# Input convolution of a two-layer decoder step: part of the taps moved from VectorE and TensorE to ScalarE and GpSimd

## The reference, cut to what matters

```python
def conformer_conv(h, buf, w_in, w_dw, b_dw, ln_g, ln_b, w_out):
    a, gate = jnp.split(h @ w_in, 2, axis=-1)
    u = a * jax.nn.sigmoid(gate)
    u, tail = causal_depthwise_conv(u, buf, w_dw, b_dw)   # width 31, 1024 channels
    u = layernorm(u, ln_g, ln_b)
    return jax.nn.silu(u) @ w_out, tail
```

## Time and profile before

| | us |
|---|---|
| median of 3 runs (lowest, highest) | 1561.69 (1561.35, 1566.02) |
| the profiled execution's own time | 1561.86 |
| its span, first to last instruction | 1560.1 |
| TensorE busy | 1502.1 (96%) |
| VectorE busy | 1014.5 (65%) |
| ScalarE busy | 879.0 (56%) |
| GpSimd busy | 138.4 (9%) |
| mean granted TensorE clock | 0.994 |

### The profile page before, as it was taken

One profiled execution on the slowest core, in us unless ns is written; L12 is line 12 of the kernel. 1 busy time (PEld: TensorE's weight loads), 2 busy tenths in 40 slices (PEclk: granted clock), 3 DMA queues, 4 the chain that ended last, 5 costly groups with the idle time before them and its releaser, 6 DMA issues.

```text
span 1560.1 us, 28415 instructions
## 1 busy us (share of the span) xinstructions
PE 1502.1 (96%) x11348; PEld 1363.8 (87%) x11348; DVE 1014.5 (65%) x1531; ACT 879.0 (56%) x1625; POOL 138.4 (9%) x364
## 2 busy tenths in 40 slices
PE   5999999999999999999999998999999999999997
PEld 4777746999999999999979966668999999999996
DVE  5999984778664597654627435664688654676743
ACT  4465466677653576643515545664686653566632
POOL 1000000000000132200000012210000000232200
PEclk9999999999999999999999999999999999999998
DMA  9765485135454344554427246665145554454553
GB/s 366 289 242 229 151 315 192 60 123 173 164 187 167 133 163 162 175 189 142 135 81 274 98 162 222 219 221 169 41 149 176 162 195 158 135 175 163 192 168 98
DMA packets 71764, 273.76 MB, mean 175 GB/s; under 512 B 8032, under 2 KB 10096, under 8 KB 71120
## 3 DMA queue, kind: packets, MB, share of 16 engines
q1 hardware_dynamic: 65248, 246.44, 46.2%
q0 software_dynamic: 6096, 25.15, 4.9%
q10 hardware_dynamic: 288, 0.35, 0.1%
HBM read 262.80 MB, written 8.85 MB: 174 GB/s over the span
## 4 chain that ended last, share of the span: by engine, by line
PE 80%; DVE 10%; ACT 3%; issue 3%; DMA 2%; SPq 1%; DVEq 0%; ACTq 0%
PE ps L678 59%; PE ps L917 4%; PE ps L655 3%; DVE w_lo L1571 2%; PE ps L751 2%; DVE odd_taps L1748 2%; DVE y L1748 2%; PE ps L728 1%; PE ps L953 1%; PE ps L970 1%; PE ps L976 1%; PE ps L1037 1%; SPq L572 1%; PE ps L989 1%; DVE y L1862 1%
## 5 line engine op out<-in xcount | busy, mean ns | idle before, releaser
L678 PE MATMUL ps<-h_hi,w_hi 128*128 128x288 f32 x1920 | 571.4, 298 | 10.7 <-DVE w_lo L1571 8.3
L678 PE MATMUL ps<-h_lo,w_hi 128*128 128x288 f32 x1920 | 565.3, 294 | 0.0
L678 PE MATMUL ps<-h_hi,w_lo 128*128 128x288 f32 x1920 | 565.3, 294 | 0.0
L1571 DVE TENSOR_TENSOR w_lo<-raw,w_hi 128x1024 fp32r<-128x1024 f32 (+1 forms) x309 | 403.1, 1306 | 232.4 <-ACT w_hi L1166 231.9
L1166 ACT ACTIVATE w_hi<-raw 128x1024 fp32r<-128x1024 f32 (+1 forms) x309 | 346.7, 1123 | 108.6 <-PE ps L678 73.1
L678 PEld LDWEIGHTS ps<-h_hi,w_hi 128*128 128x128 f32 x1920 | 360.1, 188 | 19.0 <-DVE w_lo L1571 11.4
L678 PEld LDWEIGHTS ps<-h_lo,w_hi 128*128 128x128 f32 x1920 | 360.1, 188 | 0.9
L678 PEld LDWEIGHTS ps<-h_hi,w_lo 128*128 128x128 f32 x1920 | 360.0, 188 | 0.0
L678 PE MATMUL ps<-act_hi,w_hi 128*128 128x288 f32 x704 | 208.3, 296 | 0.0
L678 PE MATMUL ps<-act_lo,w_hi 128*128 128x288 f32 x704 | 207.7, 295 | 0.0
L678 PE MATMUL ps<-act_hi,w_lo 128*128 128x288 f32 x704 | 207.0, 294 | 0.0
(11 more groups left out here) (243 smaller groups left out, 1956.1 us busy)
## 6 DMA issues: line engine op xcount, KB each, us to landing
raw<-w_k_dram SPq DMA_DIRECT2D x245, 512.0 KB, 3.5
raw<-w_down_dram SPq DMA_DIRECT2D x64, 704.0 KB, 4.1
ada_w<-w_ada_dram SPq DMA_DIRECT2D x71, 512.0 KB, 5.4
k_page<-cache_kt_dram SPq DMA_DIRECT2D x32, 512.0 KB, 5.4
v_page<-cache_v_dram POOLq DMA_DIRECT2D x32, 512.0 KB, 5.3
ada_h<-w_ada_dram SPq DMA_DIRECT2D x7, 512.0 KB, 13.7
ada_u<-w_ada_dram SPq DMA_DIRECT2D x6, 512.0 KB, 15.6
ada_g<-w_ada_dram SPq DMA_DIRECT2D x6, 512.0 KB, 5.8
```

The costliest lines, as they stand in the source:

```text
L678: mm = pe.matmul(ps[:, BANK[b], 0:HALF], lhsT=w[s][:, kb * P:(kb + 1) * P], rhs=v[:, at, :] if down else v[:, at, lo:hi], start=(at == 0 a ...
L1571: dve.tensor_tensor(w_lo[s][:, 0:cols], raw[n % RING][:, 0:cols], w_hi[s][:, 0:cols].bitcast(F32), ALU.subtract).then_inc(s_lo, 1)
```

## The change

The 31 taps of chunks 0 to 6 are shared anew: ScalarE makes 12 products, GpSimd adds them up (11 additions) into `y`, VectorE does 19 taps, TensorE none. Chunk 7 has 12 taps on TensorE, 10 products, 9 taps on VectorE. The products go through a ring of four buffers, `tap_prod`; `pool_tap` counts GpSimd's additions, and a product waits until the one four before it has been read. VectorE's two accumulators lie in PSUM banks 4 and 5 instead of SBUF; its last two instructions of a chunk put the total into `tap_sum` in SBUF, and GpSimd adds that to `y` during the next chunk (`LATE_SUM`, `conv_summed`). The first ten diagonals of chunk 7 are made two at a time in loops 1 to 5. TensorE's taps go to bank 1.

```diff
-PE_TAPS = [0] + [6] * (C - 3) + [7, 16]
-DIAG_TILE = 7
-EARLY_TAPS = [22] + [18] * (C - 3) + [6, 0]
+PE_TAPS = [0] * (C - 1) + [12]
+POOL_TAPS = [12] * (C - 1) + [10]
+DVE_TAPS = [WA - n - m for n, m in zip(PE_TAPS, POOL_TAPS)]
+PRODS = 4
+POOL_DONE = [sum(n - 1 for n in POOL_TAPS[:i]) for i in range(C + 1)]
+PROD_READ = [POOL_DONE[i] + max(n, 1) for i in range(C) for n in range(POOL_TAPS[i])]
+DIAG_TILE = 10
+EARLY_TAPS = [13] + [9] * (C - 3) + [2, 0]
+DVE_STEPS = [n + 1 for n in DVE_TAPS[:-1]] + [DVE_TAPS[-1] + 2]
+LATE_SUM = 5
...
@@ TensorE: conv_taps, the block loop, mean_sum
                 pe.wait_ge(diag_made, DIAGS[i])
-                if i >= 2:
-                    pe.wait_ge(taps, TAP_DONE[i - 2])
...
-                if b % 2:
-                    both_halves(b)
-                else:
-                    both_halves(b, range(C // 2))
-                    if PE_TAPS[b // 2 - 1]:
-                        conv_taps(b // 2 - 1)
-                    both_halves(b, range(C // 2, C))
+                both_halves(b)
...
-                pe.wait_ge(taps, TAP_DONE[n])
+                if n < C - 1:
+                    pe.wait_ge(conv_summed, n + 1)
+                else:
+                    pe.wait_ge(taps, TAP_DONE[n])
@@ ScalarE
+            def tap_products(i, part):
+                if part.start == 0:
+                    act.wait_ge(pair_free[1], i + 1)
+                for n in part:
+                    k, g = PE_TAPS[i] + n, sum(POOL_TAPS[:i]) + n
+                    if g >= PRODS:
+                        act.wait_ge(pool_tap, PROD_READ[g - PRODS])
+                    act.activation(tap_prod[g % PRODS][:], u_p[:, i, k:k + TP], ACT.Copy, scale=prm("w_a_dw", i * WA + k))\
+                        .then_inc(prod_made, 1)
...
-                for k in range(min(PE_TAPS[i], DIAG_TILE)):
...
+                if i in range(1, 6):
+                    for k in range(2 * i - 2, 2 * i):
...
                 if i:
-                    seq_products(i - 1, range(0, ahead))
+                    tap_products(i - 1, range(0, 4))
+                    seq_products(i - 1, range(0, 10))
+                    tap_products(i - 1, range(4, 6))
                 split_ahead(2 * i + 1)
                 if i:
-                    seq_products(i - 1, range(ahead, WA))
-            seq_products(C - 1, range(0, WA))
+                    seq_products(i - 1, range(10, 20))
+                    tap_products(i - 1, range(6, 8))
+                    seq_products(i - 1, range(20, WA))
+                    tap_products(i - 1, range(8, POOL_TAPS[i - 1]))
+            tap_products(C - 1, range(0, 4))
+            act.wait_ge(gemm_done, 2 * C)
+            for k in range(DIAG_TILE, PE_TAPS[C - 1]):
...
+            for n in range(4, POOL_TAPS[C - 1]):
+                seq_products(C - 1, range(4 * (n - 4), 4 * (n - 3)))
+                tap_products(C - 1, range(n, n + 1))
@@ VectorE: tap
-                out = odd_taps[:] if odd else whole
+                out = ps[:, 4 + odd, :]
...
+                    if i < C - 1:
+                        dve.tensor_tensor(tap_sum[:], ps[:, 5, :], tap_sum[:], ALU.add).then_inc(taps, 1)
+                    elif n == DVE_TAPS[i]:
+                        dve.wait_ge(pool_tap, POOL_DONE[i + 1])
+                        dve.tensor_tensor(y[:, i, 0:TP], ps[:, 4, :], y[:, i, 0:TP], ALU.add).then_inc(taps, 1)
...
+                    if i < C - 1 and n >= DVE_TAPS[i] - 2 and not odd:
+                        to = tap_sum[:]
+                        if i:
+                            dve.wait_ge(conv_summed, i)
@@ GpSimd, ahead of its wait for glu(7) and the two stores
+            for i in range(C):
+                out = y[:, i, 0:TP]
+                for n in range(1, POOL_TAPS[i]):
+                    g = sum(POOL_TAPS[:i]) + n
+                    pool.wait_ge(prod_made, g + 1)
+                    if n > 1:
+                        pool.wait_ge(pool_tap, POOL_DONE[i] + n - 1)
+                    pool.tensor_tensor(out, tap_prod[(g - 1) % PRODS][:] if n == 1 else out, tap_prod[g % PRODS][:], ALU.add)\
+                        .then_inc(pool_tap, 1)
+                    if i and n == LATE_SUM:
+                        pool.wait_ge(taps, TAP_DONE[i - 1])
+                        pool.tensor_tensor(y[:, i - 1, 0:TP], y[:, i - 1, 0:TP], tap_sum[:], ALU.add).then_inc(conv_summed, 1)
```

More of the change, by code:

```diff
@@ L63 @@
 RING = 3
-PE_TAPS = [0] + [6] * (C - 3) + [7, 16]
-DIAG_TILE = 7
-EARLY_TAPS = [22] + [18] * (C - 3) + [6, 0]
+PE_TAPS = [0] * (C - 1) + [12]
[6 more added lines that the diff above has]
+EARLY_TAPS = [13] + [9] * (C - 3) + [2, 0]
 TURNS_FROM = [1] * (C - 1) + [3]
-TAP_DONE = [sum(WA - n + 1 for n in PE_TAPS[:i + 1]) for i in range(C)]
+DVE_STEPS = [n + 1 for n in DVE_TAPS[:-1]] + [DVE_TAPS[-1] + 2]
+TAP_DONE = [sum(DVE_STEPS[:i + 1]) for i in range(C)]
+LATE_SUM = 5
 PE_SUMS = [sum(n > 0 for n in PE_TAPS[:i + 1]) for i in range(C)]
@@ L369, in trunk_kernel @@
         u_s = place("u_s", [P, C, NS, WA - 1 + TS], at=at)
-        diag = [place(f"diag{s}", [P, DIAG_TILE, P], at=at) for s in range(2)]
+        diag = place("diag", [P, DIAG_TILE, P], at=at)
+        tap_sum = place("tap_sum", [P, TP], at=at)
         ada_w = [place(f"ada_w{s}", [P, C * P], at=at) for s in range(ADA_RING)]
@@ L398, in trunk_kernel @@
         h_first = place("h_first", [P, 2, TP], at=temp())
+        tap_prod = [place(f"tap_prod{j}", [P, TP], at=temp(NS * TS * WA * 4 + j * TP * 4)) for j in range(PRODS - 1)]
         c_raw = place("c_raw", [P, C, NB], at=temp())
@@ L404, in trunk_kernel @@
         c_act = place("c_act", [P, C, 32], at=at)
+        tap_prod.append(place(f"tap_prod{PRODS - 1}", [P, TP], at=list(at)))
         sq_ln = [place("sq_ln0", [P, TT], at=temp(shared)), place("sq_ln1", [P, TT], at=at)]
@@ L746, in conv_taps @@
                 pe.wait_ge(diag_made, DIAGS[i])
-                if i >= 2:
-                    pe.wait_ge(taps, TAP_DONE[i - 2])
                 for k in range(PE_TAPS[i]):
-                    d = diag[i % 2][:, k, :] if k < DIAG_TILE else diag_more[:, k - DIAG_TILE, :]
-                    mm = pe.matmul(ps[:, 4 + i % 2, :], lhsT=d, rhs=u_p[:, i, k:k + TP],
+                    d = diag[:, k, :] if k < DIAG_TILE else diag_more[:, k - DIAG_TILE, :]
+                    mm = pe.matmul(ps[:, TAP_BANK, :], lhsT=d, rhs=u_p[:, i, k:k + TP],
                                    start=(k == 0), stop=(k == PE_TAPS[i] - 1))
@@ L848, in _ @@
             late_pieces(len(OWN_TILE))
-            for n in range(C):
+            for n in range(C - 1):
                 mean_sum(n, 0)
-                if n < C - 1:
-                    mean_sum(n, 1)
+                mean_sum(n, 1)
+            mean_sum(C - 1, 0)
             late_pieces(ADA_RING)
@@ L1725, in tap @@
             def tap(i, n):
-                g, k, turn = TAP_DONE[i - 1] if i else 0, PE_TAPS[i] + n, TURNS_FROM[i]
-                whole, odd = y[:, i, 0:TP], n >= turn and (n - turn) % 2 == 0
-                out = odd_taps[:] if odd else whole
-                if k == WA:
+                g, k, turn = TAP_DONE[i - 1] if i else 0, PE_TAPS[i] + POOL_TAPS[i] + n, TURNS_FROM[i]
+                odd = n >= turn and (n - turn) % 2 == 0
+                out = ps[:, 4 + odd, :]
+                if n >= DVE_TAPS[i]:
                     dve.wait_ge(taps, g + n)
-                    dve.tensor_tensor(whole, whole, odd_taps[:], ALU.add).then_inc(taps, 1)
+                    if i < C - 1:
[3 more added lines that the diff above has]
+                        dve.tensor_tensor(y[:, i, 0:TP], ps[:, 4, :], y[:, i, 0:TP], ALU.add).then_inc(taps, 1)
+                    else:
+                        dve.tensor_tensor(y[:, i, 0:TP], ps[:, 5, :], y[:, i, 0:TP], ALU.add).then_inc(taps, 1)
                     return
@@ L1802, in _ @@
             split_ahead(2 * C - 1)
-            early_taps(C - 1, range(0, WA - PE_TAPS[C - 1] + 1))
+            early_taps(C - 1, range(0, DVE_STEPS[C - 1]))
             dve.wait_ge(mod_ready, GROUPS - 2)
```

25 lines of the change are left out of this document (11 added, 14 removed).

## The result

| | before | after |
|---|---|---|
| median (lowest to highest), us | 1562.91 (1561.35 to 1566.02), 4 runs | 1550.05 (1548.80 to 1552.90), 4 runs |
| profiled execution's own time | 1561.86 | 1548.80 |
| span | 1560.1 | 1547.2 |
| TensorE busy | 1502.1 | 1469.0 (95%) |
| VectorE busy | 1014.5 | 987.7 (64%) |

The ratio after to before is 0.9923, with a 95% interval of 0.9904 to 0.9942: faster by 0.8%, 13 us. The time lies 3.5 us above the 1546.6 predicted, inside the range. The gauge of the prediction (the end of the first 15 sums of the mean) moved from 229.02 to 216.62, by 12.4, and the execution's own time by 13.06: what moved in the stage arrived at the end.

The account below looks back on a forecast made before the run. TensorE and VectorE were taken as both full from 48 to 199 us. Relieving both moves the end of the mean's first 15 sums from 229.0 to 213.9; 1561.86 - 15.1 = 1546.8, median 1546.6, range 1539 to 1558.

Parts of the forecast that it names:

- an addition, from start to start: GpSimd, each chunk: 1.2 us per addition, between bounds 0.60 and 1.85; twelve take 14.4 us, hidden under VectorE's 18.3.
- hindrance, a chunk: VectorE's two `w_lo` meeting GpSimd's additions: 0.5 us for each `w_lo`, 10 of them in the five middle chunks.
- from there to the last diagonals: ScalarE, from the sixth sequence sum through remaining products of chunks 6 and 7 to `diag_more`: 18.0 us, so 190.0.
- cold taps of chunk 7: TensorE's twelve taps after its pause, starting at the lower clock: 10.3 us plus 2.5 lost.
- If an instruction with its accumulator in PSUM costs the same: VectorE's taps: 0.66 us each in PSUM as in SBUF, bounds 0.54 and 0.74, giving 18.3 us a chunk.
- the tail: From the sixth sequence sum to the end of the mean's first 15 sums: 41.9 us instead of 38.0.
- ScalarE: ScalarE's work per chunk: 17.7 us against 13.0 before, just fitting under VectorE's 18.3.
- Block 15: TensorE, relieved of 32 us of taps ahead of it, ends block 15 near 166 and no longer bounds the stage.
- The cost put at nothing: Convolution-state stores leaving GpSimd's queue later, when `ada_g` are fetched: costed at nothing, at up to 4 us.
- Rival D: Gain doesn't arrive: first chunk unmoved, stores delay `ada_g` and weights; 4 + 3 + 4 of 15 go; 1557 to 1558; chance 0.08.
- rival A: No hindrance: `w_lo` wait for nothing, GpSimd never holds ScalarE; 5.0 + 1.8 less, 1539.8; chance 0.14.
- rival B: Dearer PSUM taps, or each `w_lo` waiting out whole additions (port rule in full): 1554 to 1556, both 1562; chance 0.18.

## Why the prediction was right

By its own steps, predicted and measured:

| step | predicted | measured |
|---|---|---|
| first sequence sum ends | 74.5 | 75.28 |
| a tap in PSUM | 0.66 | 0.66 |
| an addition, from start to start | 1.2 | 1.42 |
| hindrance, a chunk | 1.0 | 1.04 (without additions 18.69, with 19.73); 4.9 over the ten `w_lo` of the five chunks |
| five chunks from there | 97.5 | 98.8 |
| sixth sequence sum ends | 172.0 | 174.06 |
| from there to the last diagonals | 18.0 | 18.8 |
| cold taps of chunk 7 | 12.8 | 12.56 |
| gauge | 213.9 | 216.62 |

**The mechanism** was right: work had to leave both engines at once, and the chunk became VectorE's at 19.7. Of the 2.7 us by which the gauge missed, 0.8 lie in the first chunk, 1.3 in the five, 0.8 ahead of the last diagonals, and the cold taps gave 0.2 back.

**The mis-sized terms.** "If an instruction with its accumulator in PSUM costs the same" holds for the 0.66 taps and fails for the one that opens the first accumulator: 0.46 in SBUF, 0.71 in PSUM, 0.25 a chunk, 1.3 over the five. The earlier trace rows had shown it shorter than its neighbours, and I had used it as a bound without asking why it was. The Trainium skill has a reason (VectorE: DVE Perf Modes, Why PSUM operands drop a tier): the faster mode of a single-input instruction takes both of VectorE's SBUF read ports, and so is not to be had with an operand in PSUM. The trace agrees with that in one more detail: with the accumulators in SBUF, the one that opens `odd_taps` took 0.48 alone and 1.52 at 81.20, beside a GpSimd at work.

**An addition** lasts 1.28, inside the bounds of 0.60 and 1.85 and near the 1.2 taken; the chain of `pool_tap` adds 0.14 between two. Twelve are 17.0, not 14.4, which left 2.7 us of cover in 19.7 before meetings, not 4. GpSimd held ScalarE in seven places for 3.5 us in all, and 13 products are too many; the sum of the prediction had a term for the first only in the tail (1.8 of the 4.1) and put the second too far away, at 1.9 an addition.

**ScalarE** was put at 17.7 a chunk. From one sigmoid to the next it took 18.1 to 18.7 in the last four chunks, with 0.61 instead of 0.58 for a large product. It stayed under VectorE's 19.7, as the prediction needed, but was level with the 18.3 that it was compared with. (The 13.0 given for ScalarE before is 11.8 by the prediction's own terms; nothing rests on it.)

**Block 15** was said to end near 166 and ended at 169.9, with its four pieces done at 171.8. This step was wrong in two ways that partly cancel. It gave all twelve blocks from 4 to 15 a share of pieces, but blocks 14 and 15 have none, so by its own terms (two times 1.85 less) it comes to 162.5. And TensorE had more to do than the step held: waits for pieces of `ada_w`, which make three of the groups of pieces and blocks 0.9 to 1.3 longer, and three times 0.9 for the small products with `four_diag`. VectorE held it only once, for 1.0, ahead of block 15. So TensorE, too, was busy nearly throughout (97.42 of 99 us from 73 to 172), though 32 us of taps had gone, and gained on VectorE slowly: in loop 2 VectorE still waited 0.98 for it, and block 15 was done 7.5 us before VectorE took it up (169.9 against 177.42). "TensorE no longer bounds the stage" holds, with little room. The pause was 21.2, as forecast ("some 20"), since the diagonals were later by nearly as much, 3 us.

**The cost put at nothing** was nothing: the stores left GpSimd's queue at 205.87, and the `ada_g` fetches took 11.0 us to landing (5.8 before), but the own time moved by 0.7 more than the gauge. Rival D, and the up to 4 us in it, did not come. Of rival A the run without additions (one run) shows that it would have been near 1543.7 and not 1539.8; of rival B, that the port rule in full is not what the two `w_lo` pay (1.04 a chunk, where two whole additions are 2.6).

**What I undervalued** was the tail. The prediction priced it at 3.9 us more (41.9 for 38.0) and it cost 4.6 (from 174.06 to 216.62 is 42.6), but only the experiments show what that meant: 6 us were to be had by moving two diagonals, and 9 in all by sharing chunk 7 anew as well.

## What to carry to other kernels

When two engines are both full, relieve both in one change, and test that reading by relieving each alone. A slower engine that takes over work is best used a little under its limit: here one product more, 13 instead of 12, made VectorE wait for ScalarE and ScalarE for GpSimd, and cost ScalarE the lead that the work at the end had drawn on. Before moving work in front of a small instruction, look who waits for that instruction; here two diagonals of 0.3 to 0.4 us kept a 12 us piece of TensorE's work waiting.

## What else the runs showed

- VectorE and GpSimd, each with two SBUF inputs, take turns and do not share: a tap of 0.66 then costs 1.7, a `w_lo` of 1.22 up to 2.3, an addition of 1.28 on average 1.61. With the accumulator in PSUM the same taps cost 0.66 beside a busy GpSimd.
- The opening instruction of the first accumulator costs 0.25 more in PSUM than in SBUF, while the two-input taps cost the same in both.
- TensorE's granted clock was already at 0.50 when it resumed behind pauses of 8.0 us and more. Behind the pause of 2.0 in the kernel before it was still 1.00 and fell a microsecond later:

```profile
202.00:203.00 1.00, 0.68 (x2) 0.47 (x3) 1.00 (x3) 1.00 (x5) 0.00 (x0) 1.00 1.06 389
203.00:204.00 1.00, 1.00 (x2) 0.35 (x2) 1.00 (x3) 1.00 (x6) 0.00 (x0) 0.54 1.01 291
```

  The loss did not grow with the pause: against 10.3 at full clock, twelve taps took 12.7 behind 8.0 (181.51 to 194.20), 13.6 behind 18.3 (with 10 products), 12.56 behind 21.2 and 12.3 behind 28.4 (with 13). With the pieces in between, when the whole tail was shared anew, no gap was longer than 1.8 us, and the clock stayed at 1.00.
